# A two-block language-model layer on one core: state-space input merged with setup, narrow products by features, stick-breaking logits in two row halves

## The chip, the cores and the metric

One core of one Trainium2 chip runs one program. Its engines are PE (TensorE, matrix products), DVE (VectorE), ACT (ScalarE), POOL (GpSimd) and SP (SyncE, here only a DMA queue). They work side by side and meet by semaphores. The metric is the time of one execution on the device, in microseconds. Lower is better.

## The reference, cut to what matters

The input is one sequence of 512 tokens of width 1024, all in 32-bit floats. It passes a state-space (Mamba 2) layer, an MLP, a stick-breaking attention layer, an MLP, and then a second kind of block with an RWKV branch, a sparse-attention branch with an index that chooses keys, a merge and a gated MLP.

```python
def mamba2_mixer(u, w_in, conv_w, conv_b, dt_bias, a_log, d_skip, norm_w, w_out):
    zxbcdt = u @ w_in                       # 1024 x (2048 + 4096 + 32)
    z = zxbcdt[..., :D_INNER]
    xbc = zxbcdt[..., D_INNER:D_INNER + CONV_DIM]
    dt_raw = zxbcdt[..., D_INNER + CONV_DIM:]          # 32 columns, one per head
    xbc = jax.nn.silu(causal_depthwise_conv(xbc, conv_w, conv_b))
    ...
    dt = jax.nn.softplus((dt_raw + dt_bias).astype(jnp.float32))
    a = -jnp.exp(a_log.astype(jnp.float32))
    y = ssd_chunked_scan(xh * dt[..., None], dt * a, bm, cm)

def stick_breaking_attention(u, w_q, k, v, w_o):       # 16 heads of 64
    z = jnp.einsum("bhqd,bhkd->bhqk", qi, kj)          # the logits
    ...

# second block: w_in_2 gives, among others, 512 + 64 + 8 index columns:
q_idx, k_idx, w_idx = jnp.split(p_idx, ci, axis=-1)
q_idx = rope(...); k_idx = rope(...)
```

## The kernel before

**Phases.** `build` makes a list of phases and each engine runs its part of each in order. After a phase whose name is not in `flowing` all four engines meet (`phase_done`). The first phases are `setup`, `mamba_in` and `mamba_scan`, with a meeting after each. Later come `sb_project`, `sb_attend` and, after an MLP, `second_front`.

**Weights and products.** A large product is a `Gemm`. Its weight is cut into chunks of 256 rows by at most 512 columns (`KC` = 2 tiles of 128 rows). SP loads the chunks in one fixed order through a ring of 4, POOL splits each into a high and a low part (lines 409 and 412) in a ring of 6, and PE multiplies. Each product is three matmuls: high by high, low by high, high by low. With `feature=True` the weight is the stationary operand and the 512 tokens stream, so the result has features on the partitions. With `feature=False` a block of 128 tokens is stationary and the weight's columns stream. `part` yields after each tile of a chunk, and a full round is 6 matmuls. Line 153 of the profile is the matmul by features, line 155 the one by tokens. Results stand in 8 PSUM banks, and `tile_free` counts tiles that have been read.

**setup** (line 734). POOL fills constants. PE turns the 512 x 1024 input in 8 steps (line 779), ACT copies the high part, DVE subtracts for the low part. SP loads 4 pieces of the input, 4 weight chunks and then 16 small parameter rows. PE turns the parameter rows (lines 784 and 785), and ACT copies them to `par_cols`. Then comes the first meeting.

**mamba_in** (line 815). `g` is the 4096-column product by features: 8 parts of 4 tiles, 4 chunks each. For each tile DVE makes the convolution in 4 instructions (lines 871, 873 twice, 875) and ACT the Silu (line 909). After part j PE turns the four tiles of part j-1 (`turn`, line 846). ACT makes `turned(n - 4)` (a copy, line 904) right after the Silu of tile n, and PE uses two PSUM banks for the turned tiles in alternation. After the 8 parts comes `gd`, 32 columns by tokens: 96 matmuls of 32 columns. Then a chain runs through DVE, ACT and PE that makes the time steps and the decay sums (lines 879 to 923), and then the meeting before `mamba_scan`, whose first matmul is line 960.

**sb_attend** (line 1193). For each head, `logits` is four 32-bit matmuls with 64 contraction rows, for key blocks 2 and 3, then 1, then 0, of 256, 128, 384 and 512 columns. Each shows as two records. Head h has its queries and keys on partitions 0 to 63 when h is even, 64 to 127 when it is odd, so all the logits of one head stand in one half of the rows. ACT takes Abs of the three spans, then Exp and Ln (`ln`), DVE adds, PE adds sums (`exponents`), and ACT takes Exp. The PE order is logits(h+1), for odd h also `out` for a pair of heads, then exponents(h). The logits of head h+2 wait span by span for the last Exp of head h (`s_w`), whose banks they reuse.

**second_front** (line 1409). `gi` makes 584 index columns by tokens: a part of 512 columns and one of 72. ACT copies both into `idxTok`. DVE rotates each of 4 token blocks (6 instructions on 288 columns, lines 1790 to 1795, and a copy, line 1856), waiting only for that block's tile of the second part. PE goes on with `ga` (`qkv`) for 8 rounds, then turns one block after the other with 2 rounds after each (`turn_index`, line 1504), and then starts the index products (`index_pair`, line 1521), which are pairs of matmuls on the two row halves.

## Time and profile before

| | us |
|---|---|
| median of 3 runs | 2640.85 |
| lowest, highest | 2638.74, 2643.32 |
| the profiled execution's own time | 2641.31 |
| span of its trace | 2639.5 |
| PE busy | 2490.9 (94%) |
| mean granted clock of PE | 0.964 |

The span is what the trace covers, and about 1.8 us of the execution's own time lies around it. PE is TensorE's matmuls, PEld its weight loads. In a timeline row the first number is the start in us from the start of the span, the second how long the group lasted, "x" how many instructions are in it, and the bracket the idle time of the engine before it and what ended it. The granted clock is a share of full speed. A line number points into the kernel before, and one that belongs to a helper stands for all its calls.

### The profile page before, as it was taken

The numbers are of one execution on the slowest core, as the hardware profiler recorded it, in microseconds if no ns is written. First come the engines' busy times: TensorE is split into PE (matmuls) and PEld (weight loads), VectorE is DVE, ScalarE is ACT, GpSimd is POOL, SyncE is SP. The second block draws the span as 40 slices with busy tenths as digits, with TensorE's granted clock in tenths as the row PEclk, the third lists the DMA queues.
The fourth block names the chain that finished last, engine by engine and source line by source line (L and its number), as shares of the span: only waits on it lengthen the run. The fifth ranks groups of instructions, "written<-read, shape, count | busy, mean of one in ns | idle before, by whom it ended". The sixth has DMA issues, their size and how long they took to land.

```text
span 2639.5 us, 34935 instructions
## 1 busy us (share of the span) xinstructions
PE 2490.9 (94%) x14538; PEld 2019.2 (77%) x14538; DVE 1003.8 (38%) x1619; ACT 571.3 (22%) x1155; POOL 1494.0 (57%) x1396
## 2 busy tenths in 40 slices
PE   8998998999999999999999998998688998999998
PEld 6777886788888888558888887675477687888887
DVE  3443748155033400334512435775632332421023
ACT  1112322012011011760201101345443210110010
POOL 7554556568587486335867746471121664666663
PEclk9997999999999999999999998999798999999999
DMA  5222022223233233002332322130000232333321
GB/s 170 72 58 72 1 73 88 88 94 105 82 104 102 61 121 101 8 16 89 104 96 93 99 64 87 45 96 24 1 4 3 92 96 72 104 96 96 96 80 64
DMA packets 104290, 199.07 MB, mean 75 GB/s; under 512 B 9306, under 2 KB 12612, under 8 KB 104132
## 3 DMA queue, kind: packets, MB, share of 16 engines
q1 hardware_dynamic: 101476, 189.36, 23.0%
q10 hardware_dynamic: 2656, 7.47, 0.8%
q8 instruction: 115, 1.88, 0.3%
q14 instruction: 43, 0.35, 0.0%
HBM read 194.71 MB, written 2.10 MB: 75 GB/s over the span
## 4 chain that ended last, share of the span: by engine, by line
PE 84%; DVE 9%; ACT 3%; POOL 2%; issue 2%; SPq 0%; DMA 0%; DVEq 0%; POOLq 0%; ACTq 0%
PE psum L153 35%; PE psum L293 23%; PE psum L155 8%; PE psum L232 3%; PE psum L1253 1%; POOL weight_split_ring L412 1%; PE psum L968 1%; PE psum L1262 1%; PE psum L194 1%; DVE big L873 1%; PE psum L982 1%; PE psum L1281 1%; DVE big L1821 1%; DVE best L1820 1%; POOL weight_split_ring L409 0%
## 5 line engine op out<-in xcount | busy, mean ns | idle before, releaser
L412 POOL TENSOR_TENSOR weight_split_ring<-weight_ring,weight_split_ring 128x512 fp32r<-128x512 f32 (+2 forms) x732 | 953.6, 1323 | 30.6
L153 PE MATMUL psum<-x_split,weight_split_ring 128*128 128x512 f32 x4080 | 958.5, 394 | 1.9 <-POOL weight_split_ring L412 1.3
L153 PEld LDWEIGHTS psum<-x_split,weight_split_ring 128*128 128x128 f32 x4080 | 766.8, 189 | 171.9 <-issue 11.6
L409 POOL TENSOR_SCALAR weight_split_ring<-weight_ring 128x1024 fp32r<-128x1024 f32 (+2 forms) x366 | 395.2, 1080 | 735.2 <-PE psum L293 340.7
L293 PE MATMUL psum<-weight_split_ring,hidden_split 128*128 128x512 f32 x2448 | 576.6, 396 | 8.2 <-DVEq L2931 8.2
L293 PEld LDWEIGHTS psum<-weight_split_ring,hidden_split 128*128 128x128 f32 x2448 | 460.4, 188 | 120.0 <-DVEq L2931 8.6
L155 PE MATMUL psum<-weight_split_ring,x_split 128*128 128x512 f32 (+2 forms) x1056 | 240.5, 388 | 2.0 <-DVEq L2931 1.4
L155 PEld LDWEIGHTS psum<-weight_split_ring,x_split 128*128 128x128 f32 x1056 | 196.8, 207 | 44.5 <-issue 7.2
L708 DVE TENSOR_TENSOR big<-big 128x512 f32<-128x512 f32 x64 | 88.7, 1386 | 179.6 <-ACT big L693 179.6
L511 DVE SCALAR_TENSOR_TENSOR residual<-residual,psum 128x512 f32<-128x512 f32 x48 | 32.8, 683 | 262.2 <-PE psum L293 262.2
L693 ACT ACTIVATE big<-psum 128x512 f32<-128x512 f32 x64 | 38.3, 598 | 434.9 <-PE psum L153 378.9
L1336 DVE SCALAR_TENSOR_TENSOR big<-psum,big 128x384 f32<-128x384 f32 (+1 forms) x48 | 27.3, 596 | 197.4 <-ACT big L1309 197.4
L446 DVE SCALAR_TENSOR_TENSOR residual<-residual,psum 128x512 f32<-128x512 f32 x24 | 16.5, 687 | 213.7 <-PE psum L293 213.7
L232 PE MATMUL psum<-x_split,weight_split_ring 128*128 128x256 f32 x768 | 95.7, 284 | 1.6 <-POOL weight_split_ring L412 1.4
L232 PEld LDWEIGHTS psum<-x_split,weight_split_ring 128*128 128x128 f32 x768 | 93.3, 191 | 2.7 <-POOL weight_split_ring L412 2.0
L293 PE MATMUL psum<-weight_split_ring,x_split 128*128 128x512 f32 x384 | 89.8, 395 | 3.5 <-DVEq L2931 3.5
L2711 DVE TENSOR_TENSOR big<-big,psum 128x512 f32<-128x512 f32 x22 | 15.1, 688 | 196.0 <-PE psum L153 196.0
L710 DVE TENSOR_TENSOR hidden_split<-big,hidden_split 128x512 fp32r<-128x512 f32 x64 | 87.5, 1368 | 2.2
L293 PEld LDWEIGHTS psum<-weight_split_ring,x_split 128*128 128x128 f32 x384 | 72.9, 191 | 19.2 <-DVEq L2931 4.0
L577 ACT ACTIVATE deviation<-mean_square 128x1 f32<-128x1 f32 x24 | 4.9, 203 | 360.8 <-DVE mean_square L522 360.8
L2357 POOL TENSOR_TENSOR big<-big,pair_masks 128x512 f32<-128x512 f32 x20 | 26.8, 1345 | 91.9 <-PE psum L2101 54.5
L871 DVE TENSOR_SCALAR big<-psum,parameter_columns 128x512 f32<-128x512 f32 x32 | 25.8, 805 | 121.3 <-PE psum L153 121.3
(327 smaller groups left out, 2504.1 us busy)
## 6 DMA issues: line engine op xcount, KB each, us to landing
weight_ring<-in_mlp_w SPq DMA_DIRECT2D x128, 512.0 KB, 3.6
weight_ring<-in_w_in SPq DMA_DIRECT2D x92, 512.0 KB, 3.6
weight_ring<-in_w_ffn_in SPq DMA_DIRECT2D x40, 512.0 KB, 3.5
weight_ring<-in_w_out SPq DMA_DIRECT2D x24, 512.0 KB, 3.6
weight_ring<-in_w_ffn_out SPq DMA_DIRECT2D x22, 512.0 KB, 3.5
weight_ring<-in_sb_w_q SPq DMA_DIRECT2D x8, 512.0 KB, 3.6
weight_ring<-in_sb_w_k SPq DMA_DIRECT2D x8, 512.0 KB, 3.7
weight_ring<-in_sb_w_v SPq DMA_DIRECT2D x8, 512.0 KB, 3.6
```

The lines of the kernel that those rows point to most:

```text
L153: mm = pe.matmul(out, wp[:, k, m * P:(m + 1) * P], xp, start=first, stop=last)
L155: mm = pe.matmul(out, xp[:, m * P:(m + 1) * P], wp[:, k, 0:n], start=first, stop=last)
L232: mm = pe.matmul(out, wp[:, k, m * P:(m + 1) * P], xp[:, cols], start=first, stop=last, skip_group_check=True)
L293: mm = pe.matmul(out, xp[:, t * P:(t + 1) * P], wp[:, k, :], start=first and k == 0 and q == 0, stop=last and k == nk - 1 and q == 2)
L409: pool.tensor_scalar(part.high[:, 0:nk, 0:n], raw, 1.0, 0.0, ALU.mult, ALU.add).then_inc(self.high_made, 1)
L412: low = pool.tensor_tensor(part.low[:, k, 0:n], raw[:, k, :], part.high[:, k, 0:n].bitcast(F32), ALU.subtract)
L511: dve.scalar_tensor_tensor(out=hs, in0=hs, scalar=self.alpha, in1=ps, op0=ALU.mult, op1=ALU.add)\
L693: act.activation(m.relu_tmp[:, n % 2, :], ps, ACT.Relu).then_inc(kit.tile_free, 1)
L708: step(dve.tensor_tensor(sq, r, r, ALU.mult))
L710: dve.tensor_tensor(m.hid.low[:, n % HALF, :], sq, m.hid.high[:, n % HALF, :].bitcast(F32), ALU.subtract)\
L1336: step.mark(dve.scalar_tensor_tensor(out=sp, in0=kit.psum[:, 3 * (h % 2) + bk, 0:w], scalar=0.0, in1=sp, op0=ALU.max, op1=ALU.add))
L2357: pool.tensor_tensor(m.level[s], m.kb[s], across(m.pair_mask[:, 1 + lv, 0:64], HEADS), ALU.mult)\
```

## The change

**setup and mamba_in are one phase.** There is no meeting between them. PE turns the input, then starts the first part of the product (`g0`, 4 tiles) and turns the parameter rows after 8 of its 16 rounds. The 32 dt columns come next (`gd`, 4 rounds), and then the other 28 tiles (`g1`, 7 parts). Inside the first part of `g1` stand `turn_dt` (before round 2), `decay_sums` (before round 6) and four turned tiles. Inside the later parts four turned tiles stand at rounds 4, 7, 10 and 13. ACT does four Silus, then in later parts first four copies of turned tiles and then four Silus. DVE and ACT make the time steps between tile 3 and tile 4.

**Narrow products by features.** `gd` (32 columns) and a new `gj` (the last 72 index columns) have `feature=True`. Each is 24 matmuls of 512 streamed columns instead of 96 of 32 or 72. The result is turned back by PE (`turn_dt`, `turn_narrow`) after a copy by ACT, and ACT copies it again. In `second_front` DVE's rotation of every block now waits for that last copy.

**Stick-breaking logits in both row halves.** From head 2 on, key blocks 1, 2 and 3 are computed from a copy of queries and keys in the other 64 partitions (`m.swap`), block 0 from the own half. The copies are DMAs issued by ACT, two for each pair of heads: for pairs 1 and 2 before the first `ln`, for pairs 3 to 7 after `ln(h + 1)` of an even h, two pairs ahead.

```diff
-            kit.tiles += n // P if feature else NT
+            kit.tiles += -(-n // P) if feature else NT
...
-                            mm = pe.matmul(out, wp[:, k, m * P:(m + 1) * P], xp, start=first, stop=last)
+                            mm = pe.matmul(out, wp[:, k, m * P:m * P + rows], xp, start=first, stop=last)
...
+    g0 = Gemm(kit, w_in, KD, D_INNER, WIDE, True, banks=BK)
+    gd = Gemm(kit, w_in, KD, D_INNER + XBC, SSM_HEADS, True, banks=BK)
+    g1 = Gemm(kit, w_in, KD, D_INNER + WIDE, XBC - WIDE, True, banks=BK)
...
+        def turn_dt():
+            gd.wait_free(pe, 0)
+            pe.wait_ge(s_xh, PARAMETERS)
+            for c in range(NT):
+                mm = pe.transpose(kit.psum[:, 7, c * SSM_HEADS:(c + 1) * SSM_HEADS], m.dt_rows[:, c * P:(c + 1) * P],
+                                  m.ident[0:SSM_HEADS, 0:SSM_HEADS])
+            mm.then_inc(s_xt, 1)
+
+        def decay_sums():
+            pe.wait_ge(s_dt, DA)
+
+            pe.wait_ge(m.constants_cut, CONSTANT_STEPS)
...
+        def turn(n):
+            pe.wait_ge(s_silu, n + 1)
+            if n < 2:
+
+                pe.wait_ge(s_dt, TO_END)
+            else:
+                pe.wait_ge(s_tf, n - 1)
...
+        pe.wait_ge(s_sel, 1)
+        for n in range(2 * NT):
+            turn_x(n)
+        pe.wait_ge(s_xl, 2 * NT)
+        go_on(first, 8)
+        turn_parameters()
+        go_on(first, 8)
+        go_on(small, ROUNDS // NT)
+        for j in range(len(g1.parts)):
+            at = [9, 11, 13, 15] if j == 0 else [4, 7, 10, 13]
+            for r in range(ROUNDS):
+                if j == 0 and r == 2:
+                    turn_dt()
+                if j == 0 and r == 6:
+                    decay_sums()
+                if r in at and 4 * j + at.index(r) < TURNED:
+                    turn(4 * j + at.index(r))
+                go_on(wide, 1)
...
+        for n in range(NT):
+            conv(n)
+        time_steps()
+        for n in range(NT, XBC_TILES):
+            conv(n)
...
+        def time_steps():
+            act.wait_ge(s_par, LANDED)
+            act.activation(m.head_rows[:, 1, :], m.head_rows[:, 1, :], ACT.Exp).then_inc(s_exp, 1)
+            g0.wait_free(act, NT - 1)
+            act.activation(m.dt_rows, gd.wait_tile(act, 0)[0:SSM_HEADS, :], ACT.Copy).then_inc(kit.tile_free, 1)
...
+        for n in range(NT):
+            silu(n)
+        time_steps()
+        for n0 in range(NT, XBC_TILES, NT):
+            for n in range(n0 - NT, min(n0, TURNED)):
+                turned(n)
+            for n in range(n0, n0 + NT):
+                silu(n)
...
+                    if n == 0:
+                        pe.wait_ge(s_sw[(h // 2) % 2], 32 * ((h // 2 + 1) // 2))
                 for b in blocks:
-                    mm = pe.matmul(bank(h, b), m.kF[rows(h), h // 2, b * P:(b + 1) * P], m.qF[rows(h), h // 2, b * P:],
-                                   start=(b != 3), stop=True, skip_group_check=True)
+                    if h >= 2 and b >= 1:
+                        k, q = other_k(h, b), other_q(h, b)
+                    else:
+                        k, q = m.kF[rows(h), h // 2, b * P:(b + 1) * P], m.qF[rows(h), h // 2, b * P:]
+                    mm = pe.matmul(bank(h, b), k, q, start=(b != 3), stop=True, skip_group_check=True)
...
+        def copy_halves(p):
+            if p >= 3:
+
+                act.wait_ge(s_z, NS * (2 * p - 2))
+            for g in range(2):
+                act.dma_start(m.swap[rows(g + 1), p % 2], m.qkF[rows(g), :, p, P:]).then_inc(s_sw[p % 2], 16)
+
...
-    gi = Gemm(kit, w_in, KD, RW_COLS + 3 * ATT, IDXW, False)
+    gi = Gemm(kit, w_in, KD, RW_COLS + 3 * ATT, ATT, False)
+    gj = Gemm(kit, w_in, KD, RW_COLS + 4 * ATT, IDXW - ATT, True)
...
-        go_on(qkv, 8)
-
-        gi.wait_free(pe, gi.count - 1)
+        for _ in gj.stream(pe, m.x_tile):
+            pass
+        go_on(qkv, 2)
+        turn_narrow()
+        go_on(qkv, 6)
...
+        act.activation(m.kidx[0:NARROW, :], gj.wait_tile(act, 0)[0:NARROW, :], ACT.Copy).then_inc(kit.tile_free, 1)
+        act.wait_ge(s_tr, 1)
+        act.activation(m.idxTok[:, :, ATT:IDXW], kit.psum[:, 5, 0:NT * NARROW].rearrange("p (t c) -> p t c", t=NT),
+                       ACT.Copy).then_inc(s_tf, 1)
...
+        dve.wait_ge(s_tf, 1)
         for t in range(NT):
 
-            gi.wait_free(dve, NT + t)
             step(rotate(t, m.idxTok[:, t, 0:ATT + HD], NHEAD + 1))
```

## Rows read from the trace of the kernel before

**Rows 1.** The page, busy time of each engine.

```profile
PE 2490.9 (94%) x14538; PEld 2019.2 (77%) x14538; DVE 1003.8 (38%) x1619; ACT 571.3 (22%) x1155; POOL 1494.0 (57%) x1396
```

**Rows 2.** Windows; columns as in its first line, the granted clock before the last two.

```profile
core 0: us, PE busy (x) PEld busy (x) DVE busy (x) ACT busy (x) POOL busy (x), PEclk, DMA share, GB/s
...
17.80:23.00 5.20, 5.15 (x12) 4.10 (x13) 0.00 (x0) 0.00 (x0) 4.95 (x5) 0.50 0.43 111
...
227.80:253.50 25.70, 17.99 (x85) 17.75 (x85) 8.22 (x17) 7.08 (x12) 14.47 (x13) 0.50 0.35 103
...
1627.20:1640.80 13.60, 13.60 (x59) 12.92 (x59) 6.57 (x5) 0.92 (x4) 13.27 (x12) 0.51 0.52 152
```

**Rows 3.** Timeline of PE, 0 to 256 us: start, length, what, idle before.

```profile
17.85 46.37 PE L153 MATMUL psum<-x_split,weight_split_ring 128*128 128x512 f32 x192 [0.54 <-ACTq L2931]
64.06 1.03 PE L846 MATMUL psum<-constants,big 128*128 128x128 f32 x8
...
121.45 22.04 PE L153 MATMUL psum<-x_split,weight_split_ring 128*128 128x512 f32 x96
...
173.26 23.63 PE L153 MATMUL psum<-x_split,weight_split_ring 128*128 128x512 f32 x96
...
253.55 0.79 PE L960 MATMUL psum<-big 128*128 128x128 f32 x2 [3.45 <-DVEq L2931]
```

**Rows 4.** Groups of PE, 0 to 256 us: busy, mean ns, idle before.

```profile
L153 PE MATMUL psum<-x_split,weight_split_ring 128*128 128x512 f32 x768 | 182.9, 401 | 0.5 <-ACTq L2931 0.5
L155 PE MATMUL psum<-weight_split_ring,x_split 128*128 128x32 f32 x96 | 17.6, 338 | 0.3 <-DVE big L875 0.3
L846 PE MATMUL psum<-constants,big 128*128 128x128 f32 x96 | 14.3, 283 | 11.9 <-ACT big L904 7.9 <-ACT residual L904 4.0
```

**Rows 5.** Timeline of all engines, first and last part of `mamba_in`.

```profile
10.89 2.49 POOL L412 TENSOR_TENSOR weight_split_ring<-weight_ring,weight_split_ring 128x512 fp32r<-128x512 f32 x2
...
232.74 0.63 ACT L909 ACTIVATE big<-big 128x512 f32<-128x512 f32 x1 [2.44 <-DVE big L875]
...
242.43 1.08 DVE L883 SCALAR_TENSOR_TENSOR heads_by_token<-heads_by_token 128x128 f32<-128x128 f32 x1
...
243.87 1.28 ACT L916 ACT_TABLE_LOAD   x1
```

**Rows 6.** Groups of DVE, 17 to 254 us.

```profile
L871 DVE TENSOR_SCALAR big<-psum,parameter_columns 128x512 f32<-128x512 f32 x32 | 25.8, 805 | 121.3 <-PE psum L153 121.3
...
L875 DVE SCALAR_TENSOR_TENSOR big<-psum,parameter_columns,big 128x509 f32<-128x509 f32 x32 | 23.9, 748 | 1.1
```

**Rows 7.** Timeline of all engines in `sb_attend`.

```profile
1078.80 1.34 ACT L1325 ACTIVATE big<-psum 128x384 f32<-128x384 f32 x3
...
1079.33 2.42 PE L1253 MATMUL psum<-big 64*128 64x256 f32 x8
...
1081.79 0.60 ACT L1303 ACTIVATE big<-psum 128x512 f32<-128x512 f32 x1 [0.37 <-PE psum L1253]
```

**Rows 8.** Timeline around 573 us: a DMA issued by ACT's queue.

```profile
572.98 0.45 ACTq L613 DMA_DIRECT2D gain_rows<-in_ln_mlp_b  x1
```

**Rows 9.** Groups of PE, 1600 to 1665 us.

```profile
L155 PE MATMUL psum<-weight_split_ring,x_split 128*128 128x72 f32 x96 | 15.6, 342 | 0.0
```

**Rows 10.** Timeline of all engines in `second_front`.

```profile
1634.16 1.25 DVE L1790 TENSOR_TENSOR big<-big,heads_by_token 128x288 f32<-128x288 f32 x1 [23.08 <-ACT big L1634]
...
1642.53 0.45 DVE L1790 TENSOR_TENSOR big<-big,heads_by_token 128x288 f32<-128x288 f32 x1
...
1650.20 0.60 PE L1504 MATMUL psum<-constants,big 128*128 128x128 f32 x4
...
1656.13 0.17 DVE L1856 COPY index_weights<-big 128x8 f32<-128x8 f32 x1
...
1665.31 0.49 PE L1521 MATMUL psum<-heads_by_token,gain_rows 64*128 64x128 f32 x4
...
1691.95 1.13 PE L1521 MATMUL psum<-heads_by_token,gain_rows 64*128 64x512 f32 x4
```

More of the change, by code:

```diff
@@ L134, in part @@
         kit = self.kit
-        tiles = n // P if self.feature else NT
+        tiles, rows = -(-n // P) if self.feature else NT, min(P, n) if self.feature else P
         for b, (k0, nk) in enumerate(blocks):
@@ L731, in load_parameters, with more_constants, mamba_in @@
         sp.dma_start(m.head_rows[:, n, :], ap.partition_broadcast(P)).then_inc(m.parameter_rows_landed, 16)
-def setup(nc, kit, m, a):
+CONSTANT_STEPS = 7
+def more_constants(kit, m, pool):
+    cut = Chain(pool, m.constants_cut)
+    for t, sign, b in ((m.upper, 1, 0), (m.upper_strict, 1, -1), (m.neg_lower, -1, 0)):
+        cut.mark(pool.affine_select(out=t[:, :], in_=t[:, :], compare_op=ALU.is_ge, fill=0.0, base=b,
+                                    pattern=[[sign, P]], channel_multiplier=-sign))
+    cut(pool.tensor_scalar(m.ident_r, m.ident, 1.0, 0.0, ALU.mult, ALU.add))
+    cut(pool.tensor_scalar(m.past_r, m.upper, -FAR, FAR, ALU.mult, ALU.add))
+    cut(pool.memset(m.halves[0:64, 0:64], 1.0))
+    cut(pool.memset(m.halves[64:P, 64:P], 1.0))
+    assert cut.n == CONSTANT_STEPS
+def mamba_in(nc, kit, m, a):
+    BK = 6
+    w_in = a["w_in"]
+    g0 = Gemm(kit, w_in, KD, D_INNER, WIDE, True, banks=BK)
+    gd = Gemm(kit, w_in, KD, D_INNER + XBC, SSM_HEADS, True, banks=BK)
+    g1 = Gemm(kit, w_in, KD, D_INNER + WIDE, XBC - WIDE, True, banks=BK)
+    TURNED = X_TILES + SSM_GROUPS
+    ROUNDS = 16
     s_base = kit.sem("constant_filled")
@@ new lines, in mamba_in, with tile, gemm, x_block @@
+    RAW, ABS, DA, TO_END = 1, 2, 3, 4
+    SUMS_READ, WEIGHT = 4, 5
+    PARAMETERS, TURNED_DT, SUMS = 2 * NT + 1, 2 * NT + 2, 2 * NT + 3
+    LANDED = 16 * (len(ROWS) + 4)
+    nrow = sum(n for _, n in ROWS)
+    def tile(n):
+        return m.xring[:, n % 8, :] if n < X_TILES else m.bcF[:, n - X_TILES, :]
+    def gemm(n):
+        return (g0, n) if n < NT else (g1, n - NT)
+    def x_block(n):
+        t, j = n // 2, n % 2
+        return t, slice(4 * j, 4 * j + 4), slice(t * P, (t + 1) * P)
@@ new lines, in tensor, with go_on, turn_x, turn_parameters @@
+    def tensor(pe):
+        first, small, wide = (g.stream(pe, m.x_tile) for g in (g0, gd, g1))
+        def go_on(stream, n):
+            for _ in range(n):
+                next(stream)
+        def turn_x(n):
+            t, feats, _ = x_block(n)
+            if n % 2 == 0:
+                pe.wait_ge(m.x_landed[t], 16)
+            if n >= 4:
+                pe.wait_ge(s_xl, n - 3)
+            for q in range(4):
+                f = feats.start + q
+                mm = pe.transpose(kit.psum[:, n % 4, q * P:(q + 1) * P], m.h[:, t, f * P:(f + 1) * P], m.ident[:, :])
+            mm.then_inc(s_xt, 1)
+        def turn_parameters():
+            pe.wait_ge(s_par, LANDED)
+            pe.transpose(kit.psum[:, 7, 0:nrow], m.par_rows[0:nrow, 0, :], m.ident[0:nrow, 0:nrow])
+            pe.transpose(kit.psum[:, 7, P:2 * P], m.par_rows[:, 1, :], m.ident[:, :]).then_inc(s_xt, 1)
+        def turn_dt():
[4 more added lines that the diff above has]
+                                  m.ident[0:SSM_HEADS, 0:SSM_HEADS])
+            mm.then_inc(s_xt, 1)
+        def decay_sums():
+            pe.wait_ge(s_dt, DA)
+            pe.wait_ge(m.constants_cut, CONSTANT_STEPS)
+            for c in range(NT):
+                pe.matmul(kit.psum[:, 7, c * 32:c * 32 + 32], m.upper[:, :], m.da[:, c, :], start=True, stop=True)
+                mm = pe.matmul(kit.psum[:, 7, P + c * 32:P + c * 32 + 32], m.ones[:, :], m.da[:, c, :], start=True, stop=True)
+            mm.then_inc(s_xt, 1)
+        def turn(n):
[4 more added lines that the diff above has]
+                pe.wait_ge(s_tf, n - 1)
+            for c in range(NT):
+                mm = pe.transpose(kit.psum[:, BK + n % 2, c * P:(c + 1) * P], tile(n)[:, c * P:(c + 1) * P],
+                                  m.ident[:, :])
+            mm.then_inc(s_tr, 1)
+        pe.wait_ge(s_sel, 1)
[16 more added lines that the diff above has]
+                go_on(wide, 1)
@@ L1199, in sb_attend @@
     s_z = kit.sem("sb_logits_ready")
+    s_sw = [kit.sem(f"sb_other_half_landed{n}") for n in range(2)]
     s_soft = kit.sem("sb_last_abs_then_exp_then_ln_ready")
@@ L1314, in scalar @@
                 ln(h + 1)
+            if h % 2 == 0 and 2 <= h <= SB_HEADS - 6:
+                copy_halves(h // 2 + 2)
             if h >= 3 and h % 2 == 1:
@@ L1493, in go_on, with turn_narrow @@
                 next(stream)
+        def turn_narrow():
+            gj.wait_free(pe, 0)
+            for t in range(NT):
+                mm = pe.transpose(kit.psum[:, 5, t * NARROW:(t + 1) * NARROW], m.kidx[0:NARROW, block(t)],
+                                  m.ident[0:NARROW, 0:NARROW])
+            mm.then_inc(s_tr, 1)
         def turn_index(t):
@@ L2785, in __init__ @@
         self.bcF = self.part(b, 0, 2 * SSM_GROUPS, SEQ)
+        self.dt_rows = self.part(b, 14 * SEQ, SEQ)[0:SSM_HEADS, :]
         self.past_r = self.hid.low[:, 8, 0:P]
```

251 lines of the change are left out of this document (97 added, 154 removed).

## The prediction, made before the changed kernel ran

> **What bounds the kernel now.** I read the page first: PE is busy 94% of the span, no other engine over 57% [rows 1]. So time comes back only where PE idles, where it runs at its lower clock, or where it has fewer or shorter instructions. The windows by stage came next, for the clock. In three of the stages that the change touches PE runs at half speed (0.50, the 1.2 GHz level): after the first start, all through `gd` and the chain behind it, and during the 72-column part of the index product [rows 2]. Both narrow products keep PE busy with short matmuls, and the clock falls during each. The timeline of PE then shows the stretches of `mamba_in`: start at 17.85, the first turned tiles at 64.06, a part of 96 matmuls in 22.04 us, another in 23.63, and the scan's first matmul at 253.55 [rows 3]. So a wide matmul costs 22.04/96 = 0.23 us and a round of six 1.38. The groups say that the turned tiles waited 11.9 us in all and that `gd` took 17.6 + 0.3 us [rows 4].
>
> **The change part by part, first the merged phase.**
>
> 1. Start. PE started at 17.85, after the parameter rows and the meeting. Now it needs only the input's low parts and the first split chunk, done at 10.89 + 2.49 = 13.38 [rows 5]. That gives 4.5. The parameter turn moves into the stream, some 0.5 (eight turned blocks took 1.03 [rows 3]). Net 4.0. The half-speed stretch after the start should be as long as before, so it cancels.
> 2. Turned tiles. The 24 turns keep their work and lose their waits of 11.9 us [rows 4], if each finds its Silu and bank ready. A tile's convolution takes about 0.8 + 3 x 0.75 = 3.05 us on DVE [rows 6] and its Silu 0.63 [rows 5]. The first turned tile of a part stands at round 4 of the next, and needs one tile more than itself: two convolutions and a Silu, 6.7 us, after round 12. That is round 12 to round 20, 8 x 1.38 = 11 us. The cover is 4 us. The copies in runs are then covered too. If the cover went, PE would pay the excess at each turn.
> 3. Clock. 768 wide matmuls at 0.23 would take 176.3, and took 182.9 [rows 4]. The start's stretch explains 2.4 of the 6.6 (12 matmuls in 5.2 us where 22.6 fit [rows 2]), the rest is stretches after waits, like the part of 23.63. Without waits the rest of 4.2 comes back.
> 4. `gd`: 17.9 becomes 24 x 0.23 = 5.5. Gain 12.4.
> 5. The chain after `gd`. DVE began it at 242.43 [rows 5] and the scan started at 253.55 [rows 3], so 11.1 go. PE still makes `turn_dt` (0.5) and 16 small passes for the decay sums: at 1.03/8 each 2.1, at half speed 4.1; I take 3.0. Their inputs have cover: from `turn_dt` to `decay_sums` are 4 rounds, 5.5 us, against some 4.2 for DVE and ACT (1.08 and 1.28 are the two long pieces [rows 5], five short ones of 0.3 to 0.5 beside them). Later 3 rounds, 4.1 us, cover a table load and five short pieces, 2.9.
> 6. A new wait at `turn_dt`. From the end of `g0` PE needs 6 rounds, 8.3 us. ACT must first do four Silus. Tile 0 is ready 3 rounds before the end, four convolutions take 12.2, so the last Silu ends 12.2 - 4.1 + 0.63 = 8.7 after `g0`. Then a table load of 1.28, an Exp of 0.25, and a copy of 512 columns, 0.6: 10.9, with semaphores 11.1. PE waits 2.8. Queued behind it are only PE's own rounds. The clock probably falls once after it, 1.6 (the two parts of rows 3 compared).
> 7. A new tail. Before, `gd` covered the last four convolutions. Now the last matmul is followed by 12.2 - 4.1 + 0.63 + 0.1 = 8.9 us before the meeting is over.
>
> Sum: 4.0 + 11.9 + 4.2 + 12.4 + 11.1 - 0.5 - 3.0 - 2.8 - 1.6 - 8.9 = 26.8. Bounds: 31 with no loss of clock and short sums, 20 with four more half-speed stretches.
>
> SP loads the four `gd` chunks earlier, behind the 16 parameter rows, and POOL's constants still come after six chunks. POOL has some 3.3 us of work in a chunk (12 instructions, three a chunk, in 13.27 us [rows 2]) and PE 5.5, so nothing waits there, and these cost nothing.
>
> **Logits.** The trace of before has no run of one half followed by the other. The nearest row is a pair of index matmuls on the two halves, four passes of 512 columns in 1.13 us [rows 10]. The eight logit passes, 2560 columns in one half, take 2.42 [rows 7], by which those 2048 columns would take 1.94. So the halves do run side by side. For a head, block 0 can run beside block 1 at most (two passes of 384, 0.73 us), and not before the third Exp has freed its bank, 0.81 after the logits began [rows 7], which leaves 0.64. But ACT waited only 0.37 for the logits' end before its third Abs [rows 7], having just finished the second. What the logits save beyond that doesn't reach ACT, whose chain sets the pace in every other head: the logits at 1079.33 started when the first of its Exps, begun at 1078.80, was done. I take 0.37 for each of 14 heads, 5.2 us. Bounds: 0 and 14 x 0.64 = 9.0.
>
> The Trainium skill's page "TensorE: Matmul & The Clock Gate", section "Part 3: Packing small matmuls", says that matmuls start and end strictly in program order. Read so, block 0's first pass could start beside the last pass of block 1 only, 0.36 a head. The pair's row, full overlap, would give the upper bound. The whole would differ by 3.8 us, and this page speaks for my value.
>
> The two DMAs of a pair are issued by ACT's queue, 0.45 us each by the nearest row [rows 8]. They stand behind Ln, and its 1.3 us cover 0.9, since the queue can run ahead of the engine. Without that cover they cost 5 x 0.9 = 4.5. They are issued three heads ahead of their use, and the logits of three heads alone take 7.3 us, so I expect no wait for the landing. The four before the first `ln` lie beside the table load and the slow first logits.
>
> **Index product.** On PE, 15.6 us [rows 9] become 5.5, gain 10.1; some 3 us of the next matmuls leave the half-speed stretch (until 1640.8 [rows 2]), 1.5; the narrow turn costs 0.5. PE reaches the first turned block at 1650.2 - 11.1 = 1639.1 instead of 1650.2 [rows 10]. But it needs DVE's rotation. This starts when the turned narrow part is copied, near 1631.4, against 1634.16. The first rotation took 8.3 us, while POOL was splitting chunks (13.27 of 13.6 us busy [rows 2]), and its instructions 1.25 us and more; the next one's took 0.45 [rows 10] with POOL idle. All four ended at 1656.3 [rows 10]. A faster PE frees chunks earlier, so POOL is busy until about 1650 without a pause. With 3 to 3.5 rotation instructions in each chunk of just under 4 us, the four rotations end near 1640, 1648.5, 1652.5 and 1657.5. PE waits at each turned block, most at the second (near 5 us). The last turn and its 2 rounds take (1665.31 - 1650.20)/4 = 3.8, so the index products start at 1661.4 instead of 1665.31. Gain 3.9. Bounds: 11.1 when rotations never hold PE; a loss of 3.6 when all four take 8.4 us.
>
> **Sum.** 26.8 + 5.2 + 3.9 = 35.9. The profiled execution took 2641.3 (a span of 2639.5 and 1.8 around it), so 2605.4. It stands 0.5 above the median of the three runs, so against that 2604.9. I say 2605.
>
> **Rivals.**
>
> - The halves don't overlap, because of the semaphore wait between block 1 and block 0, or ACT's issues cost what the halves give. For it: no row shows this order. Against: the pair's row. 2605 + 5 = 2610. Chance 0.14.
> - The rotations don't hold PE, since DVE gets more gaps between POOL's instructions than I count. For it: the second rotation's 0.45. Against: POOL has no pause. 2605 - 7 = 2598. Chance 0.10.
> - The clock. The wait at `turn_dt`, the 32-column sums, and waits at the turned index blocks each bring half-speed stretches, five of 1.6: 2613. For it: both narrow stretches of rows 2. Against: they are short here. Chance 0.14.
> - Slower. In `mamba_in` each turned tile waits for a convolution and a Silu, 3.05 + 0.63 = 3.7, if DVE falls behind. 24 x 3.7 = 89 us would make 2694. It decides from (35.9 + 5.3)/24 = 1.7 us a turn. Against: DVE has 12.2 us of work for a part of 22, and 4 us of cover. Chance 0.03.
> - Two of the first three together, 2590 to 2620: 0.05.
>
> My own forecast has 0.54.
>
> **How the numbers follow.** About 0.2%, 5.3 us, is what a measurement of this kernel can tell from no change. All cases but the fourth lie well below 2635: faster 0.95, the same 0.02, slower 0.03. The range takes the bounds of the parts, not all at once: 2605 - 11 (no rotation wait, 7, and a fuller overlap, 4) and 2605 + 12 (clock 8, and no overlap or less index gain, 4). So 2594 to 2617.
>
> **What would show it.** In the trace of after: the first wide matmul near 13.4; one PE wait of about 3 us near 47; no wait before turned tiles; the scan's first matmul near 253.6 - 26.8 = 227; a `gj` of 24 matmuls in 5.5 us at full clock; PE waits before turned index blocks, released by DVE, of 6 to 8 us together; logits of one head in about 2.05 us instead of 2.42. I'm wrong if the scan starts after 233 or before 222, if PE waits at turned tiles of `mamba_in`, or if ACT's DMA issues lengthen a pair of heads.

## The result, and the profile of the changed kernel

The changed kernel takes 2603.22 us (median of 4 runs, 2602.33 to 2607.64) where the kernel before took 2640.73 (4 runs, 2638.74 to 2643.32). The ratio is 0.9868, with a 95% interval of 0.9856 to 0.988: faster by 37.5 us, or 1.3%. The prediction was 2605, with a range of 2594 to 2617. The profiled executions, on which the steps below are compared, took 2641.31 and 2602.33, a gain of 39.0.

The page of the changed kernel, busy time of each engine, against [rows 1]:

```profile
PE 2453.9 (94%) x14402; PEld 1981.2 (76%) x14402; DVE 1008.3 (39%) x1616; ACT 575.2 (22%) x1156; POOL 1496.4 (58%) x1396
```

PE has 37 us less to do and is as full as before. The mean granted clock rose from 0.964 to 0.972 of full speed. That is less time at the lower level: 2 x 0.036 x 2639.5 = 190 us before, 2 x 0.028 x 2600.5 = 146 after. PE does half as much in such a stretch, so 44 us less of it are up to 22 us of PE's time; part of those 44 us lay in idle time, where they cost nothing.

The windows of the changed kernel show where; columns as in the first line.

```profile
core 0: us, PE busy (x) PEld busy (x) DVE busy (x) ACT busy (x) POOL busy (x), PEclk, DMA share, GB/s
15.00:18.40 3.40, 3.40 (x10) 2.67 (x9) 0.00 (x0) 0.00 (x0) 3.32 (x4) 0.50 0.08 13
49.00:52.50 3.50, 3.50 (x10) 2.74 (x9) 1.21 (x4) 2.00 (x3) 3.42 (x4) 0.52 0.49 150
61.00:215.00 154.00, 152.55 (x720) 126.08 (x718) 78.07 (x105) 31.01 (x51) 94.63 (x80) 1.00 0.31 92
1586.50:1592.00 5.50, 5.50 (x26) 3.39 (x25) 0.00 (x0) 0.60 (x1) 5.42 (x5) 1.00 0.31 95
```

All that holds PE's turned tiles, 61 to 215, runs at the full level, and so does `gj`, in the place of the 72-column stretch of [rows 2] at 0.51. Up to 215, two stretches of 3.4 are left at the lower level: one after the start, one behind the wait at `turn_dt`. The same view of the kernel before had three between the turned tiles:

```profile
67.60:71.00 3.40, 3.30 (x10) 2.85 (x11) 3.27 (x5) 1.12 (x2) 0.41 (x1) 0.50 0.49 150
173.40:176.80 3.40, 3.40 (x10) 2.63 (x10) 3.29 (x5) 1.11 (x2) 0.00 (x0) 0.51 0.06 10
200.70:204.10 3.40, 3.40 (x11) 2.73 (x10) 3.29 (x5) 1.11 (x2) 0.00 (x0) 0.51 0.05 20
```

The timeline of PE in the changed kernel, 0 to 235 us, answers to [rows 3]:

```profile
13.61 12.78 PE L153 MATMUL psum<-x_split,weight_split_ring 128*128 128x512 f32 x48 [3.36 <-POOL weight_split_ring L412]
...
48.67 0.43 PE L817 MATMUL psum<-constants,big 32*128 32x32 f32 x4 [2.83 <-ACT big L933]
...
56.20 0.30 PE L827 MATMUL psum<-heads_by_token,constants 128*128 128x32 f32 x2
...
57.90 4.38 PE L153 MATMUL psum<-x_split,weight_split_ring 128*128 128x512 f32 x18
62.12 0.60 PE L839 MATMUL psum<-constants,big 128*128 128x128 f32 x4
...
222.64 0.79 PE L1010 MATMUL psum<-big 128*128 128x128 f32 x2 [9.08 <-ACTq L3021]
...
228.92 0.49 PE L1010 MATMUL psum<-big 128*128 128x128 f32 x2 [1.44 <-DVE big L1094]
```

The scan starts at 222.64 instead of 253.55, 30.9 earlier. No turned tile (L839) waits. The last row is a loss that I had not counted. The scan's first Exp now follows a Silu, so ACT loads its table there (1.28), and PE waits 1.44 for what hangs on it. One scan step later the lead is 29.8.

PE's waits from 0 to 235 us in the changed kernel: us, how many, the longest.

```profile
PE psum L1010 <- ACTq L3021: 9.1, 1, 9.1
PE psum L805 <- DMA residual<-in_x: 4.5, 1, 4.5
PE psum L153 <- POOL weight_split_ring L412: 3.4, 1, 3.4
PE psum L817 <- ACT big L933: 2.8, 1, 2.8
PE psum L1010 <- DVE big L1094: 1.4, 1, 1.4
```

These five are all. The 11.9 us of [rows 4] are not among them.

The timeline of PE and ACT around one head's logits, changed kernel, against [rows 7]:

```profile
1054.31 1.36 ACT L1398 ACTIVATE big<-psum 128x384 f32<-128x384 f32 x3
...
1054.85 1.24 PE L1316 MATMUL psum<-gain_rows 64*128 64x256 f32 x5 [0.17 <-ACT big L1398]
...
1055.72 0.69 PE L1316 MATMUL psum<-big 64*128 64x512 f32 x1
...
1055.93 0.48 PE L1316 MATMUL psum<-gain_rows 64*128 64x384 f32 x1
...
1056.26 0.59 PE L1316 MATMUL psum<-big 64*128 64x512 f32 x1
...
1056.45 1.03 ACT L1372 ACTIVATE big<-psum 128x384 f32<-128x384 f32 x2 [0.16 <-PE psum L1316]
```

The eight passes end 1.99 after they began, in every other head 1.88, against 2.42. The row of five holds both passes of blocks 2 and 3 and the first of block 1, and ends at 1056.09. Block 0's first pass, from the other half, starts at 1055.72, inside it, and **before** block 1's second pass at 1055.93. So the two halves run beside each other, and a pass of one half need not wait for both passes of the matmul ahead of it in the other. The overlap isn't quite free: block 0's second pass (1056.26) follows its first after 0.54, where in the kernel before it was 0.43. ACT's last two Abs are now one row without the gap of 0.37.

The timeline of PE in `second_front`, changed kernel, against [rows 10]:

```profile
1586.44 5.71 PE L153 MATMUL psum<-x_split,weight_split_ring 128*72 128x512 f32 x24
...
1604.36 0.66 PE L1586 MATMUL psum<-constants,big 128*128 128x128 f32 x4 [0.98 <-DVE index_weights L1944]
...
1612.64 1.12 PE L1586 MATMUL psum<-constants,big 128*128 128x128 f32 x4 [4.30 <-DVE index_weights L1944]
...
1617.89 0.60 PE L1586 MATMUL psum<-constants,big 128*128 128x128 f32 x4
...
1622.87 0.66 PE L1586 MATMUL psum<-constants,big 128*128 128x128 f32 x4 [1.07 <-DVE index_weights L1944]
...
1626.77 0.49 PE L1603 MATMUL psum<-heads_by_token,gain_rows 64*128 64x128 f32 x4
```

At the gi product (first matmul 1595.78 before, 1560.08 now) the lead over before is 35.7. When PE comes to the first of these turned blocks it has grown to 46.8 (1650.20 - 1604.36 + 0.98). Then 6.35 go into three waits, all released by the rotations on DVE, and another 1.7 into a half-speed stretch of 3.4 behind the longest wait. At the first index pair the lead is 38.5. These are PE's own times. What sets the first index pair is the last rotation: PE waits 1.07 for it at the fourth block, so without the half-speed stretch PE would, by these rows, only have waited longer there.

### The profile page after: what moved, and what is told of

Its sections match the earlier page's. It is cut to its first block, busy times and chain, and to the rows that moved or that the text cites. A ratio compares the mean times of both kernels' runs of the same rounds, so it can differ in the third digit from the quotient of the medians.

```text
span 2600.5 us, 34685 instructions
## 1 busy us (share of the span) xinstructions
PE 2453.9 (94%) x14402; PEld 1981.2 (76%) x14402; DVE 1008.3 (39%) x1616; ACT 575.2 (22%) x1156; POOL 1496.4 (58%) x1396
## 4 chain that ended last, share of the span: by engine, by line
PE 84%; DVE 9%; ACT 3%; POOL 2%; issue 1%; DMA 0%; DVEq 0%; ACTq 0%; POOLq 0%; SPq 0%
PE psum L153 37%; PE psum L293 24%; PE psum L155 6%; PE psum L232 3%; POOL weight_split_ring L412 1%; PE psum L1316 1%; PE psum L1324 1%; PE psum L194 1%; PE psum L1018 1%; PE psum L1032 1%; PE psum L1343 1%; DVE big L1909 1%; DVE best L1908 1%; POOL weight_split_ring L409 0%; DVE big L881 0%
## 5 line engine op out<-in xcount | busy, mean ns | idle before, releaser
L153 PE MATMUL psum<-x_split,weight_split_ring 128*128 128x512 f32 x4128 | 971.7, 394 | 4.7 <-POOL weight_split_ring L412 4.7
L412 POOL TENSOR_TENSOR weight_split_ring<-weight_ring,weight_split_ring 128x512 fp32r<-128x512 f32 (+3 forms) x732 | 955.0, 1325 | 30.6
L409 POOL TENSOR_SCALAR weight_split_ring<-weight_ring 128x1024 fp32r<-128x1024 f32 (+3 forms) x366 | 396.3, 1083 | 700.1 <-PE psum L293 340.5
L155 PE MATMUL psum<-weight_split_ring,x_split 128*128 128x512 f32 x864 | 205.3, 396 | 1.7 <-DVEq L3021 1.4
L155 PEld LDWEIGHTS psum<-weight_split_ring,x_split 128*128 128x128 f32 x864 | 162.1, 190 | 43.5 <-issue 7.4
L293 PE MATMUL psum<-weight_split_ring,x_split 128*128 128x512 f32 x384 | 89.8, 395 | 3.5 <-DVEq L3021 3.5
L293 PEld LDWEIGHTS psum<-weight_split_ring,x_split 128*128 128x128 f32 x384 | 72.9, 191 | 19.1 <-DVEq L3021 4.0
```

Of the source, the lines that this page charges most:

```text
L153: mm = pe.matmul(out, wp[:, k, m * P:m * P + rows], xp, start=first, stop=last)
L155: mm = pe.matmul(out, xp[:, m * P:(m + 1) * P], wp[:, k, 0:n], start=first, stop=last)
L293: mm = pe.matmul(out, xp[:, t * P:(t + 1) * P], wp[:, k, :], start=first and k == 0 and q == 0, stop=last and k == nk - 1 and q == 2)
L409: pool.tensor_scalar(part.high[:, 0:nk, 0:n], raw, 1.0, 0.0, ALU.mult, ALU.add).then_inc(self.high_made, 1)
L412: low = pool.tensor_tensor(part.low[:, k, 0:n], raw[:, k, :], part.high[:, k, 0:n].bitcast(F32), ALU.subtract)
```

## The experiments

Eleven experiments ran, in three groups, each on a chip of its own. The place where time was won or lost is told by the start of the same matmul in each trace. The whole time alone is not sharp enough for a step of 3 us: the kernel before, run again beside each group, had medians from 2635.97 to 2643.23.

**1. Logits in their own half, copies kept.** The edit:

```
-                    if h >= 2 and b >= 1:
-                        k, q = other_k(h, b), other_q(h, b)
-                    else:
-                        k, q = m.kF[rows(h), ...], m.qF[rows(h), ...]
+                    k, q = m.kF[rows(h), ...], m.qF[rows(h), ...]
```

> The stick-breaking logits all in their own row half, as before the change, while the copies into the other half and the wait for them stay (their data is not used). If it is the overlap of block 0's first pass with block 1's second that gives the gain, each head's logits take 2.42 us again instead of 1.9 to 2.0, a pair of heads 14.49 instead of 13.71, and the kernel is 14 x 0.42 = 5.9 us slower than the changed one: 2609. Rival, the copies' own issues on ACT's queue set part of the pace: then the pair of heads is longer than the 14.49 of the kernel before, and the time over 2610. Rival, no overlap, and the gain comes from elsewhere: 2603.

It took 2609.3 us. A head's logits are 2.42 again, and a pair of heads takes 14.61 us against 13.71 in the changed kernel. From ACT's timeline:

```profile
1094.38 0.60 ACT L1369 ACTIVATE big<-psum 128x512 f32<-128x512 f32 x1 [0.37 <-PE psum L1313]
...
1096.31 1.36 ACT L1375 ACTIVATE big<-big,epsilons 128x1280 f32<-128x1280 f32 x1
1096.31 1.26 ACTq L1361 DMA_DIRECT2D gain_rows<-big  x2
1097.67 1.36 ACT L1395 ACTIVATE big<-psum 128x384 f32<-128x384 f32 x3
```

The wait of 0.37 is back. The two issues (1.26) start with Ln (1.36) and end 0.10 before ACT's next instruction. One sign of the first rival is there, small: a pair is longer than the 14.49 of the kernel before, and the time stayed under its 2610. The expectation speaks of block 0's first pass beside block 1's second; by the rows above it is more than that. The sum was near all the same, and most of what comes through is ACT's wait of 0.37.

**2. Logits in their own half, no copies.** The same edit, and the three calls of `copy_halves` and the wait on `s_sw` are taken out.

> The logits in their own half and no copies at all: this part of the change undone. If the copies cost nothing in the loop, the pair of heads is 14.49 as with the copies kept. The start of the stage lost 1.45 us in the changed kernel (one more half-speed stretch, and the first Abs later). If the four copies issued there cause that, this kernel is about 1.4 faster than the one with copies kept: 2607.7; if they don't, it is 2609 as well.

2608.13 us. The pair of heads takes 14.50, so the copies' issues cost 0.11 a pair, some 0.6 in the five pairs that have them. From the stage's first logits to the gi product behind it this kernel is 5.96 us longer than the changed one: the overlap, less the copies' issues, is worth 14 x 0.42. And the start is as long as in the changed kernel (16.15 us from the first logits to head 2's, 16.14 there; 14.70 before, 13.84 with the copies kept). So the copies don't cause the slow start. The half-speed stretches fall differently there (6.8 and 6.8 long in this kernel and the changed one, 6.8 and 3.4 before, one of 10.2 with the copies kept).

**3. Index product by tokens again.** `gj`, `turn_narrow` and what belongs to them undone.

> The index product with its 72 columns by tokens again, all else as changed. My theory (PE's gain of 10 us is given back in waits for the rotations): 2.9 us slower than the changed kernel, 2606, and the first index pair 2.9 later. Rival, the rotations don't hold PE and its 10 us came through: 2613. Rival, the gain of this part is nothing: 2603.

2604.41 us. The timeline of PE:

```profile
1585.75 28.29 PE L155 MATMUL psum<-weight_split_ring,x_split 128*128 128x72 f32 x144
1613.88 0.60 PE L1577 MATMUL psum<-constants,big 128*128 128x128 f32 x4
...
1628.99 0.49 PE L1594 MATMUL psum<-heads_by_token,gain_rows 64*128 64x128 f32 x4
```

Both traces read from the start of the gi product, PE comes to its first turned block 11.3 us later than in the changed kernel, doesn't wait there, and starts the index pairs 2.97 later. So the change wins 11.3 us and gives 8.3 of them back; the forecast had 11.1 and 7.2. The whole time, 1.2 more than the changed kernel's, is too blunt to tell this from nothing (one of the four runs took 2599.69).

**4. Setup and `mamba_in` of before**, with the other two parts as changed.

> Setup and mamba_in as before the change (a separate setup, dt by tokens after the wide product, turned tiles in rows), the other two parts as changed. My theory: the parts add up; the scan's first matmul is at 253.5 again, 30.9 later, of which the scan's table load gives 1.1 back: 29.8 slower, 2633. Rival, the early part's gain is partly given back downstream by a queue (weights landing later against PE): under 2628.

2634.77 us. The scan starts at 253.67, 31.0 later, and the difference is 29.9 at the first logits and at the gi product, 30.0 at the first index pair and 30.0 at the end. Nothing of this part is given back downstream but what the scan's table load takes.

**5. All rotations in one set.** Six DVE instructions over all four token blocks in place of 24:

```
-        for t in range(NT):
-            step(rotate(t, m.idxTok[:, t, 0:ATT + HD], NHEAD + 1))
-            dve.tensor_copy(m.widx[:, t, :], m.idxTok[:, t, ATT + HD:IDXW]).then_inc(s_rot, 1)
+        step(rotate_all(m.idxTok[:, :, 0:ATT + HD], NHEAD + 1, 0))
+        dve.tensor_copy(m.widx[:, :, :], m.idxTok[:, :, ATT + HD:IDXW]).then_inc(s_rot, NT)
```

> The changed kernel with the index rotations of all four token blocks in one set of six VectorE instructions of 1152 elements (and one copy), in place of four sets of 288; they still start when the narrow part is turned, near 1595.7. My theory: while GpSimd splits chunks, a VectorE instruction waits for the end of a GpSimd one, so that their number sets the time, 1.3 to 1.5 us each whatever the size. Then six take 6 x (1.3 to 2.2), 8 to 13 us, all is rotated by 1604 to 1609, TensorE waits once, 1 to 6 us, instead of 6.35 in four places, and the first index pair comes 2 to 6 us earlier. 2597 to 2601. Rival, the time goes by the elements: 4 x 8.3 us stay 27 to 33, TensorE waits until 1623 in one piece and the kernel is 3 us or more slower (2606 or above).

2607.8 us: the time was missed, though not by the rival's mechanism. DVE and PE in this kernel:

```profile
1597.08 1.51 DVE L1891 TENSOR_TENSOR big<-big,heads_by_token 128x1152 f32<-128x1152 f32 x1 [20.23 <-ACT big L1789]
1598.51 2.44 DVE L1892 TENSOR_TENSOR big<-big,heads_by_token 128x1152 f32<-128x1152 f32 x1
...
1610.21 0.83 DVE L1955 COPY index_weights<-big 128x32 f32<-128x32 f32 x1
```

```profile
1611.10 1.12 PE L1586 MATMUL psum<-constants,big 128*128 128x128 f32 x4 [6.33 <-DVE index_weights L1955]
...
1612.77 5.10 PE L155 MATMUL psum<-weight_split_ring,x_split 128*128 128x512 f32 x12
```

All is rotated in 14.0 us instead of 27.1. Four times the elements cost 2.20 an instruction on the mean, against 1.3 to 1.5. But nothing can be turned before the last of it, PE waits 6.33 in one piece, and the half-speed stretch there, from 1607.0, is 10.2 long instead of 3.4, with 6.1 of it behind the wait (12 matmuls in 5.10 instead of 3.0). From the gi product to the first index pair it lost 0.9 against the changed kernel, and 3.1 more lie after that, where two half-speed stretches stand near 1747 and 1761 that the changed kernel's trace has not.

The rows of DVE in the changed kernel show why number counts:

```profile
1614.41 1.42 DVE L1880 TENSOR_TENSOR big<-big,heads_by_token 128x288 f32<-128x288 f32 x1
1615.75 0.44 DVE L1881 TENSOR_TENSOR big<-big,heads_by_token 128x288 f32<-128x288 f32 x1
```

The instruction at 1615.75 falls in a pause of POOL and takes 0.44, its like just before, 1.42. The two engines take turns: in experiment 5 two of POOL's instructions together took 4.6 instead of 2.5 while DVE rotated. The Trainium skill's page "SBUF — State Buffer", section "SBUF: two separate sides", has this as an exclusive lock that a VectorE instruction with two SBUF inputs and a GpSimd instruction that reads SBUF hold in turn for their whole length. These traces agree: the convolution's first instruction, which reads one operand from PSUM, took 0.80 with POOL busy as without.

**6. Wide rotations first.** As 5, but the 512 columns are rotated when gi's copies are there, the 64 after the narrow turn, and PE turns three query blocks before the first key:

```
+        gi.wait_free(dve, NT - 1)
+        rotate_all(m.idxTok[:, :, 0:ATT], NHEAD, 0).then_inc(s_rot, 1)
         dve.wait_ge(s_tf, 1)
+        step(rotate_all(m.idxTok[:, :, ATT:ATT + HD], 1, NT * NHEAD * 32))
+        dve.tensor_copy(m.widx[:, :, :], m.idxTok[:, :, ATT + HD:IDXW]).then_inc(s_rot, 1)
...
+    TURNS = [(0, 0), (1, 0), (2, 0), (0, 1), (1, 1), (3, 0), (2, 1), (3, 1)]
+    SLOTS = [[0], [1], [2, 3], [4, 5, 6, 7]]
```

> As the run before, and the 512 columns are rotated in one set as soon as their copies are there (near 1587.3), the 64 narrow ones in a second set after the narrow turn; TensorE turns three query blocks before it turns keys. If the late start of the rotations is the rest of the wait, no turned index block waits any more: the first index pair comes near 1619 instead of 1626.8, the kernel is 7 us faster than the changed one, 2596. Rival, something other than the rotations holds TensorE there (ScalarE's copies, the split chunks): waits with another releaser in the same place, and 2600 or more.

2595.87 us. No turned block waits for a rotation:

```profile
1602.63 0.60 PE L1590 MATMUL psum<-constants,big 128*128 128x128 f32 x4
...
1617.35 0.49 PE L1607 MATMUL psum<-heads_by_token,gain_rows 64*128 64x128 f32 x4
```

The stage from the gi product to the first index pair is 8.84 shorter than in the changed kernel: the waits of 6.35, the half-speed stretch of 1.7, and 0.8 of turns at full pace. So the rotations were all that held PE there. The profiled span is 7.6 shorter; behind the stage there is a half-speed stretch near 1736 that the changed kernel has not.

**7. The dt turn later.** ACT copies the dt features ahead of its fourth Silu and of the table load; `turn_dt` stands in round 3, `decay_sums` in 7, the first turned tiles in 10, 12, 14 and 15.

```
-        for n in range(NT):
+        for n in range(NT - 1):
             silu(n)
+        g0.wait_free(act, NT - 1)
+        act.activation(m.dt_rows, gd.wait_tile(act, 0)[0:SSM_HEADS, :], ACT.Copy).then_inc(kit.tile_free, 1)
+        silu(NT - 1)
         time_steps()
```

> ScalarE copies the dt features before its fourth Silu and before the table load, and TensorE turns them one round later (round 3 of 16), the decay sums in round 7, the first turned tiles in rounds 10, 12, 14, 15. My theory: the wait of 2.8 us at that turn goes, and no half-speed stretch follows it (1.7 us in those runs that show one): the scan starts 2.8 to 4.5 us earlier, 2599 to 2600. Rival, the wait only moves, to the decay sums (their inputs are then late) or to the first turned tile: 2602 to 2604.

2596.68 us, with the scan's first matmul at 217.91, 4.7 earlier. PE:

```profile
46.88 0.43 PE L817 MATMUL psum<-constants,big 32*128 32x32 f32 x4
47.24 5.74 PE L153 MATMUL psum<-x_split,weight_split_ring 128*128 128x512 f32 x24
52.82 0.30 PE L827 MATMUL psum<-heads_by_token,constants 128*128 128x32 f32 x2
```

Neither the wait nor the half-speed stretch is there, and no other wait took their place. The profiled span is 4.8 shorter. The median lies 6.5 under that of the changed kernel, more than the 2.8 to 4.5 expected, and one of the four runs took 2602.65, so the 4.7 at the scan is the figure to keep.

**8. Only block 1 from the other half** (`if h >= 2 and b == 1` in place of `b >= 1`).

> In the changed logits only block 1 is taken from the other row half; blocks 2, 3 and 0 stay in their own. By program order, block 1's first pass can then run beside block 3's second (128 columns, 0.11 us) and block 0's first beside block 1's second as before: a head's logits take some 1.78 to 1.88 us where they take 1.88 to 1.99, and up to 0.1 a head reaches ScalarE: a pair of heads 13.5 to 13.7 instead of 13.71, 0 to 1.5 us in all. Rival, switching halves costs something of its own (two switches instead of one): the pair gets longer, and 2604 or more.

2603.5 us, no difference in the whole. PE in one head:

```profile
1083.11 0.59 PE L1316 MATMUL psum<-gain_rows 64*128 64x384 f32 x1
1083.27 0.38 PE L1316 MATMUL psum<-big 64*128 64x128 f32 x2
```

Block 1's first pass, alone in the other half, starts before **both** passes of block 3 (128 columns), which stands ahead of it in the program. The expectation had let it start beside block 3's second pass at the earliest. A pair of heads takes 13.64 instead of 13.71, 0.5 us in seven pairs, and the logits still 1.88 and 1.99: block 0 waits for its bank. Switching halves twice lengthened nothing. Blocks 2 and 3 in different halves would write one PSUM bank with nothing to order them. That was not tried and stays open.

**9. The tail.** For the last four tiles ACT makes the convolution's first term, and the scan begins with the load of ACT's table:

```
+            if n >= LAST:
+                dve.wait_ge(s_first, n - LAST + 1)
+            else:
                 step(dve.tensor_scalar(acc, ps, w[3], m.col("conv_b", n), ALU.mult, ALU.add))
...
+        def first_term(n):
+            g, i = gemm(n)
+            act.activation(tile(n), g.wait_tile(act, i), ACT.Identity, bias=..., scale=...).then_inc(s_first, 1)
...
+        act.preload_act_table_set("natural_log_exp_and_others")
```

> The changed kernel with the first of the four convolution instructions of the last four tiles of mamba_in on ScalarE instead of VectorE, and the scan's table for Exp loaded at the start of its ScalarE program. The tail of 9.1 us after the last wide product is set by VectorE: four convolutions of 3.07. Without the first instruction (0.80) each has 2.27; the first must wait for ScalarE's 0.6: the last Silu ends 4 x 0.8 - 0.6 = 2.6 earlier, the tail is 6.5. The table load, which delayed the scan's first Exp (TensorE waited 1.4 for what follows it), is then beside the scan's first matmuls: 1.1 more. Together 3.7, 2599.5. Rival, VectorE waits for ScalarE in each convolution, since ScalarE has Silus between them: the tail stays over 8, and 2602.

2595.26 us:

```profile
220.04 0.80 PE L1024 MATMUL psum<-big 128*128 128x128 f32 x2 [6.59 <-ACTq L3036]
220.06 1.28 ACT L1065 ACT_TABLE_LOAD   x1
```

The tail is 6.59 where it was 9.08, 2.5 less, and PE's later wait for the first decay matrices 0.52 instead of 1.44. So the mechanism is worth 3.4, close to the 3.7 expected. The profiled span is 6.4 shorter. The other 3.0 lie where nothing was edited, up to 1.7 of them behind the scan, in the first product of `mamba_gate`, where the changed kernel has a half-speed stretch of 3.4 near 326 and this one none. The median is 9.4 below that of the changed kernel on the same chip (experiment 11) and 4.2 below the 2599.5 expected, which the edit doesn't explain.

**10. Edits 6 to 9 together**, and **11. the changed kernel again** beside it.

> Four edits on the changed kernel together: the wide rotations first, the dt turn later, the last convolutions' first term on ScalarE with the early table load, and only block 1 of the logits from the other half. They are in different stages, so they should add: 7.3 + 4.7 + 3.7 + 0.5 = 16.2, that is 2587. Rival, half-speed stretches that move with the phase of the clock, 1.7 each, take some of it: up to 2592.

> The changed kernel once more beside the two others on the same chip. The same code: 2602 to 2606, with the scan's first matmul between 221 and 224, as the half-speed stretch after the dt turn comes or stays away.

2582.6 us against 2604.65, 22 us less where 16 were expected; against the kernel before the ratio is 0.9791 (0.9775 to 0.9806). PE's waits from 0 to 235 us:

```profile
PE psum L1025 <- ACTq L3058: 6.6, 1, 6.6
...
PE psum L1025 <- DVE big L1110: 0.7, 1, 0.7
```

The scan starts 7.1 earlier than in the changed kernel (2.5 and 4.7 were due), and the stretch to the first index pair is 8.6 shorter. After that the lead grows from 17.4 to 21.2 with no edit there: the same 6936 matmuls, with PE busy at the lower level for 35.6 us in place of 43.3, which is worth up to 3.9. Over the whole span the mean granted clock is 0.977, so that 119 us (2 x 0.023 x 2579.4) are at the lower level in place of 146. So the greater part of the excess over 16 is clock, and no edit was aimed at it; what moved it is not settled. Another 1.3 is the index stage, which gained 8.6 where 7.3 were due. The changed kernel again came out as expected, its scan at 224.07, just past the edge of the forecast, with a half-speed stretch of 6.8 behind `turn_dt`.

## Why the prediction came out right, step by step

- **Start, 4.0 net.** 4.24, less 0.1 for the parameter turn. I had assumed the half-speed stretch behind it as long as before; it was 3.4 instead of 5.2, 0.9 more gain.
- **Turned tiles, 11.9.** Right. No wait is left.
- **Clock, 4.2.** The three stretches shown above cost 3 x 1.7 = 5.1, and none is left between the turned tiles: mis-sized by 0.9.
- **`gd`, 12.4**, **the chain, 11.1.** Both are gone; the 24 matmuls took 5.7 at full clock. Experiment 4 brings them back with the rest, 31.0 together.
- **`turn_dt` and the decay sums, 0.5 and 3.0.** 0.36 and 1.70 (56.20 to 57.90). I had put the sums between full and half speed, and they ran at full speed.
- **New wait at `turn_dt`, 2.8.** 2.83, released by ACT's copy as named, from 45.84 to 48.67, so near 47. The half-speed stretch behind it, 1.6, was there (1.7) in this execution. Experiment 7 took both away.
- **New tail, 8.9.** 9.08.
- **Sum of the phase, 26.8, bounds 20 and 31.** 30.9. The step that failed is the size of three small terms: decay sums (1.3), clock between the turned tiles (0.9) and at the start (0.9). They and the trifles account for some 3.0 of the 4.1. Some 0.8 of the other 1.1 is in the turned tiles and the wide matmuls between them, which I had taken as unchanged. Counted from start to start without the waits, the 96 matmuls of the turned tiles took 12.6 us before and 8.5 now, and a wide matmul at full speed 0.228 before and 0.232 now, 3 us more over 752 of them. Why the time moved between the two is not shown. Seven more executions with the same first phase put the scan between 221.2 and 224.1, that is 29.5 to 32.4 earlier than before, so the upper bound was too low as well. In two of them (221.2 and 221.8) the scan started before 222, which the prediction had named as a sign of being wrong.
- **Not in the sum: the scan's table load.** 1.1 lost, an Exp behind a Silu. I had followed the moved instructions up to the phase's end, and not asked which table ACT leaves behind.
- **Logits, 5.2.** 4.4 in the trace: 0.42 a head, 5.9, less 1.5 in a slower start. Experiment 2 shows that the copies don't cause it; it goes with the half-speed stretches there. The argument from ACT's wait of 0.37 held for most of it. The copies' issues took 1.26 for two and not 0.9, and hide under Ln but for 0.11 a pair: the other sign of being wrong, that they lengthen a pair of heads, did come, worth 0.6 us in all.
- **The page's rule.** By the Trainium skill's page "TensorE: Matmul & The Clock Gate", section "Part 3: Packing small matmuls", block 0, read pass by pass, could start beside the last pass of block 1 only. That is wrong for this case: its first pass starts 0.21 before that pass does. Read by whole matmuls the page's order would still hold in that row, since block 1's first pass (1055.61) is earlier. Experiment 8 breaks it in either reading: block 1 starts at 1083.11, block 3, ahead of it, at 1083.27. The prediction's number survived because both ways led to about 0.37.
- **Index product, 3.9.** 2.8. PE reached the first turned block 11.1 to 11.3 earlier, against 11.1. The waits were 6.35, within 6 to 8, most at the second block (4.30, "near 5"). The term that was mis-sized is the end of the last rotation. Counted from the gi product, the four rotations were to end after 44.2, 52.7, 56.7 and 61.7 and ended after 44.2, 52.5, 57.2 and 62.7; the last turn and its rounds took 3.9 instead of 3.8. That is the missing 1.1. The half-speed stretch behind the second wait, 1.7, was not in my sum either, but by these rows the wait at the fourth block took it up. Experiments 3 and 6 show both sides: 3.0 lost without the part, 8.84 more won when the rotations don't hold PE.

The parts come to 30.9 - 1.1 + 4.4 + 2.8 = 37.0. The profile's 39.0 has 2.0 more in stages that the change doesn't touch (1.3 of it by the end of `mamba_gate`). Against 35.9 the errors were +4.1, -1.1, -0.8, -1.1 and +2.0, and for the most part cancel. The mechanisms were as forecast but for the table load, but that 2605 came within 2 us is in part luck.

Of the rivals, "the rotations don't hold PE" is refuted by the waits, and "the halves don't overlap" by experiments 1 and 2. The slower one, a wait at each turned tile, did not come near: none waited. The clock's rival had the right mechanism and the wrong sign, since the changed kernel lost more half-speed stretches than it got.

## What to carry to other kernels

When an engine is made faster, ask what its next consumer was doing meanwhile: the index product gave back 8 of 11 us because DVE's rotations started no earlier, and the cure was to start the part that had no need to wait. When phases are merged, follow ACT's table past the end of the moved code. Count the clock with each wait that goes or comes: the 11.9 us of waits at the turned tiles had 5.1 more beside them in half-speed matmuls, and the 4.3 at the second index block brought 1.7. But ask of each such stretch whether a later wait takes it up, as it did there.

## What was not expected of the hardware

- The two row halves of TensorE ran as two streams. An fp32 matmul shows as two passes, and the other half's first pass began at 1055.72, between the two passes of the matmul ahead of it (1055.6, which is the end of the row of five, 1056.09, less the 0.48 of such a pass, and 1055.93). In experiment 8 it began before both (1083.11 against 1083.27).
- The same instructions with the same wait don't always draw the lower clock. The wait at `turn_dt` was 2.83 in the changed kernel and 2.84 in experiment 2. Behind the first the granted clock was 0.52 (the 1.2 GHz level), behind the second 1.00. Of nine traces with this wait seven have a half-speed stretch behind it, 3.4 long in six of them and 6.8 in one, and two have none. Experiment 2's:

```profile
47.00:56.00 9.00, 7.23 (x41) 6.20 (x41) 2.14 (x4) 3.71 (x6) 8.83 (x9) 1.00 0.55 166
```

- VectorE and GpSimd took turns by whole instructions: 288 elements took 0.44 us alone and 1.29 to 1.54 beside GpSimd, 1152 elements 2.20 beside it, and GpSimd's own went from 1.26 to 2.3. A copy of 8 columns took 0.17 and 0.90.
